# Gather of a mixture-of-experts stage: rows stored feature part by feature part, slots in two halves of 320 columns

## The reference, cut to what matters

```
def grouped_moe(x, router_w, router_bias, w_gate_up, w_down):
    scores = jax.nn.sigmoid(t @ router_w)
    ...
    h = jnp.einsum('td,edf->tef', t, w_gate_up)
    a = silu(h[..., :D_EXPERT]) * h[..., D_EXPERT:] * gates[..., None]
    y = jnp.einsum('tef,efd->td', a, w_down)
```

## Time and profile before

| | |
|---|---|
| median of 3 runs | 1055.7 us (1053.37 to 1056.87) |
| profiled execution, its own time | 1055.6 us |
| its span | 1053.8 us |
| mean granted clock of TensorE | 0.994 |
| PE busy | 1024.5 us, 97% |
| VectorE busy | 659.8 us, 63% |
| ScalarE busy | 533.5 us, 51% |
| chain that ended last | PE 87%, DVE 5% |

### The profile page before, as it was taken

How to read it: one execution, slowest core, us unless ns; L and a number is a source line. 1 busy time by engine, 2 the same in 40 slices (tenths; PEclk the granted TensorE clock), 3 DMA queues, 4 the chain that set the end, 5 groups by cost and what they waited for, 6 DMA issues and landing times.

```text
span 1053.8 us, 14257 instructions
## 1 busy us (share of the span) xinstructions
PE 1024.5 (97%) x5876; PEld 863.9 (82%) x5876; DVE 659.8 (63%) x760; ACT 533.5 (51%) x649; POOL 92.1 (9%) x75
## 2 busy tenths in 40 slices
PE   8999899999999999998999999999999999999998
PEld 8997558888888889975588888888899758999997
DVE  2105655799999571065557999996748635645644
ACT  3344423677777333444236777775458544334331
POOL 0370000000000013650000000000003100000000
PEclk9999999999999999998999999999999999999999
DMA  9900921499999539028214999994141634454441
GB/s 272 299 26 21 379 80 41 161 401 381 367 367 381 146 88 262 1 55 355 80 41 159 407 383 360 373 388 171 74 160 39 232 130 160 161 214 183 166 145 47
DMA packets 93303, 214.89 MB, mean 204 GB/s; under 512 B 25248, under 2 KB 56112, under 8 KB 82880
## 3 DMA queue, kind: packets, MB, share of 16 engines
q1 hardware_dynamic: 91456, 209.40, 55.4%
q0 software_dynamic: 1504, 2.73, 1.1%
q10 hardware_dynamic: 288, 1.98, 0.5%
HBM read 213.05 MB, written 1.05 MB: 203 GB/s over the span
## 4 chain that ended last, share of the span: by engine, by line
PE 87%; DVE 5%; SPq 3%; DMA 1%; ACT 1%; issue 1%; POOL 1%; DVEq 0%; ACTq 0%
PE bank L1095 77%; PE bank L1136 2%; DMA WE<-in_w_in 1%; SPq L526 1%; POOL QL L635 1%; PE bank L1188 1%; DVE X L1681 1%; DVE small L1673 1%; DVE X L1685 1%; PE bank L1462 1%; DVE X L1671 1%; PE bank L1170 1%; PE bank L1149 1%; PE bank L1164 1%; SPq L510 0%
## 5 line engine op out<-in xcount | busy, mean ns | idle before, releaser
L1825 DVE TENSOR_TENSOR BL<-WE,BH 128x2048 fp32r<-128x2048 f32 x120 | 273.6, 2290 | 24.7 <-ACT BH L785 22.8
L785 ACT CAST BH<-WE 128x2048 fp32r<-128x2048 f32 x120 | 228.9, 1909 | 43.8 <-PE bank L1095 43.8
L1095 PE MATMUL bank<-BH,XS_ALL 128*128 128x512 f32 x512 | 163.0, 390 | 0.0
L1095 PEld LDWEIGHTS bank<-BH,XS_ALL 128*128 128x128 f32 x512 | 96.2, 188 | 19.9
L1095 PE MATMUL bank<-BL,XS_ALL 128*128 128x512 f32 x256 | 99.6, 389 | 0.0
L635 POOL TENSOR_TENSOR QL<-WE,QH 128x2048 fp32r<-128x2048 f32 (+2 forms) x12 | 49.3, 4123 | 366.6 <-ACT QH L777 366.6
L1095 PE MATMUL bank<-WB,XT 128*128 128x512 f32 x160 | 70.4, 595 | 3.2 <-ACT XT L853 1.4
L1095 PE MATMUL bank<-XTH,WH 128*128 128x256 f32 x256 | 72.6, 284 | 0.8 <-DVE XTL L1979 0.8
L1095 PE MATMUL bank<-XTL,WH 128*128 128x256 f32 x256 | 72.4, 283 | 0.0
L1095 PE MATMUL bank<-XTH,WL 128*128 128x256 f32 x256 | 72.4, 283 | 0.0
L1136 PE MATMUL bank<-tab 128*128 128x128 f32 x492 | 62.1, 285 | 5.0 <-DMA tab<-in_tables 5.0
(11 more groups left out here) (338 smaller groups left out, 2275.4 us busy)
## 6 DMA issues: line engine op xcount, KB each, us to landing
WE<-in_exp_w_gate_up SPq DMA_DIRECT2D x80, 1024.0 KB, 7.3
WE<-in_exp_w_down SPq DMA_DIRECT2D x40, 1024.0 KB, 7.4
WE<-in_w_up SPq DMA_DIRECT2D x16, 1024.0 KB, 5.2
WE<-in_w_down SPq DMA_DIRECT2D x16, 1024.0 KB, 5.7
WE<-in_w_in SPq DMA_DIRECT2D x7, 2048.0 KB, 8.4
WE<-in_w_in SPq DMA_DIRECT2D x8, 1024.0 KB, 8.3
WB<-in_w_out SPq DMA_DIRECT2D x2, 2560.0 KB, 9.9
WE<-in_w_in SPq DMA_DIRECT2D x12, 256.0 KB, 7.6
```

The lines of the kernel that those rows point to most:

```text
L785: nc.scalar.copy(BH[b % N_PAIR][:, :], raw[b % N_RAW]).then_inc(blk_high[b % N_PAIR], 1)
L1095: ins = nc.tensor.matmul(dst, lhsT, rhs, start=first and n == 0, stop=last and n == len(pairs) - 1)
L1825: v.tensor_tensor(BL[b % N_PAIR][:, :], raw[b % N_RAW], BH[b % N_PAIR][:, :].bitcast(F32), ALU.subtract).then_inc(blk_low[b % N_PAIR], 1)
```

## The change

X1H and X1L get a layout of part k by j, so that the 128 columns that one matmul takes as weights lie side by side; ScalarE's copy and VectorE's subtraction now read X with a step of eight words. SEL's columns get a new order: two halves of 320 (groups 0 and 1 with the first 64 over slots, groups 2 and 3 with the other 64), and behind them once more the 128 over slots, for the transposes and the gates. VectorE writes SEL in four operations for each tile instead of one. The gather makes jobs `ga{k}` and `gb{k}` of 320 columns in banks 2, 3, 4, 6 and 7, with four matmuls each, instead of `g{k}` and `go`. ScalarE and VectorE evacuate each job with two operations, of 256 and 64 columns. The expert stage's waits name the new jobs.

```
-    ("g0", 2), ("g1", 3), ("g2", 4), ("g3", 2), ("g4", 3), ("g5", 4), ("g6", 2), ("g7", 3), ("go0", 6), ("go1", 7),
+    ("ga0", 2), ("gb0", 3), ("ga1", 4), ("gb1", 6), ("ga2", 7), ("gb2", 2), ("ga3", 3), ("gb3", 4),
+    ("ga4", 6), ("gb4", 7), ("ga5", 2), ("gb5", 3), ("ga6", 4), ("gb6", 6), ("ga7", 7), ("gb7", 2),
...
+SEL_HALF = N_GRP // 2 * P + P // 2
+def slot_columns(g):
+    at = 2 * SEL_HALF if g == N_GRP else g // 2 * SEL_HALF + g % 2 * P
+    return slice(at, at + P)
...
-        X1H, X1L = over("X1H", "WB", 0, [P, T, D]), over("X1L", "WB", UNIT, [P, T, D])
-        SEL = over("SEL", "XT", 0, [P, T, N_SLOT * P])
+        X1H, X1L = over("X1H", "WB", 0, [P, T, KD, P]), over("X1L", "WB", UNIT, [P, T, KD, P])
+        SEL = over("SEL", "XT", 0, [P, T, 2 * SEL_HALF + P])
...
+        def feature_blocks(t):
+            return X[:, t, :].rearrange("p (j k) -> p k j", k=KD)
...
-                    nc.scalar.copy(X1H[:, t, :], X[:, t, :]).then_inc(rows_high, 1)
+                    nc.scalar.copy(X1H[:, t, :, :], feature_blocks(t)).then_inc(rows_high, 1)
...
-                for half in range(2):
-                    for k in range(4 * half, 4 * half + 4):
-                        act.wait_ge(*full(f"g{k}", l))
-                        dst = XS_ALL[:, :].rearrange("p (g q) -> p g q", g=N_GRP)[:, :, k * P:(k + 1) * P]
-                        nc.scalar.copy(dst, bank(f"g{k}")[:, :].rearrange("p (g q) -> p g q", g=N_GRP)).then_inc(gathered, 1)
-                    act.wait_ge(*full(f"go{half}", l))
-                    nc.scalar.copy(XS[N_GRP][:, half * 512:(half + 1) * 512], bank(f"go{half}")[:, :]).then_inc(gathered, 1)
-                    selection_T(half)
+                def gather_high(k, half):
+                    job = f"g{'ab'[half]}{k}"
+                    act.wait_ge(*full(job, l))
+                    dst = XS_ALL[:, :].rearrange("p (g q) -> p g q", g=N_GRP)[:, 2 * half:2 * half + 2, k * P:(k + 1) * P]
+                    nc.scalar.copy(dst, bank(job)[:, 0:2 * P].rearrange("p (g q) -> p g q", g=2))
+                    at = k * P + half * HD
+                    nc.scalar.copy(XS[N_GRP][:, at:at + HD], bank(job)[:, 2 * P:SEL_HALF]).then_inc(gathered, 1)
+                for k in range(KD):
+                    for half in range(2):
+                        gather_high(k, half)
+                    if k % 4 == 3:
+                        selection_T(k // 4)
...
                 product(ranks[:, 2 * N_GRP:3 * N_GRP], [(ones, first_tile), (ones, second_tile)]).then_inc(*made("rank"))
-                keep_warm("g0", l, 10)
+                keep_warm("ga0", l, 10)
                 pe.wait_ge(rows_low, (l + 1) * T)
                 pe.wait_ge(sel_made, (l + 1) * T)
                 def gather(dst, k, cols):
                     return product(dst, [pair for t in range(T) for pair in (
-                        (X1H[:, t, k:D:KD], SEL[:, t, cols]), (X1L[:, t, k:D:KD], SEL[:, t, cols]))])
+                        (X1H[:, t, k, :], SEL[:, t, cols]), (X1L[:, t, k, :], SEL[:, t, cols]))])
                 def selection_T(n, block, i):
-                    return nc.tensor.transpose(tile_of(f"selT{n}", block, P), SEL[:, i % 2, (i // 2) * P:(i // 2 + 1) * P].bitcast(F32), ident)
+                    return nc.tensor.transpose(tile_of(f"selT{n}", block, P), SEL[:, i % 2, slot_columns(i // 2)].bitcast(F32), ident)
                 def slot_gates(g):
                     at = 2 * P + g * PER_GRP
                     return product(bank("selT2")[:, at:at + PER_GRP], [
-                        (SEL[:, t, g * P:(g + 1) * P].bitcast(F32), gov[:, t, :]) for t in range(T)])
+                        (SEL[:, t, slot_columns(g)].bitcast(F32), gov[:, t, :]) for t in range(T)])
                 for n in range(3):
                     pe.wait_ge(*free(f"selT{n}", l))
                 for k in range(KD):
                     half = k // 4
-                    pe.wait_ge(*free(f"g{k}", l))
-                    gather(bank(f"g{k}")[:, :], k, slice(0, N_GRP * P)).then_inc(*made(f"g{k}"))
-                    if k % 4 == 0:
-                        pe.wait_ge(*free(f"go{half}", l))
-                    ins = gather(tile_of(f"go{half}", k % 4, P), k, slice(N_GRP * P, N_SLOT * P))
-                    if k % 4 == 3:
-                        ins.then_inc(*made(f"go{half}"))
+                    for part in range(2):
+                        job = f"g{'ab'[part]}{k}"
+                        pe.wait_ge(*free(job, l))
+                        gather(bank(job)[:, 0:SEL_HALF], k, slice(part * SEL_HALF, (part + 1) * SEL_HALF)).then_inc(*made(job))
                     ins = selection_T(half, k % 4, k)
                     if k % 4 == 3:
                         ins.then_inc(*made(f"selT{half}"))
...
                     for part, kind in enumerate(("A", "B")):
                         b = BLOCK_AT[kind, n]
                         pe.wait_ge(*rested(b, l))
-                        if n == 0:
+                        if n % (2 * PER_GRP) == 0:
                             for k in range(4 * part, 4 * part + 4):
-                                pe.wait_ge(*read(f"g{k}", l))
-                        elif n == N_GRP * PER_GRP:
-                            pe.wait_ge(*read(f"go{part}", l))
+                                pe.wait_ge(*read(f"g{'ab'[n // (2 * PER_GRP) % 2]}{k}", l))
                         high, low = (w[b % N_PAIR][:, :].rearrange("p (k n) -> p k n", k=KD // 2) for w in (BH, BL))
                         for k in range(KD // 2):
                             kk = 4 * part + k
...
                     evacuate(f"x1T{n}", XT[:, 2 * n:2 * n + 2, :], l)
                 for t in range(T):
                     dve.wait_ge(rows_high, l * T + t + 1)
-                    v.tensor_tensor(X1L[:, t, :], X[:, t, :], X1H[:, t, :].bitcast(F32), ALU.subtract).then_inc(rows_low, 1)
+                    v.tensor_tensor(X1L[:, t, :, :], feature_blocks(t), X1H[:, t, :, :].bitcast(F32), ALU.subtract
+                                    ).then_inc(rows_low, 1)
                 dve.wait_ge(router_in, 32)
...
                 link(v.tensor_reduce(posm[:, :, N_GRP], posm[:, :, 0:N_GRP], AX.X, ALU.add))
                 link(v.tensor_scalar(posm[:, :, N_GRP], posm[:, :, N_GRP], float(-P), None, ALU.add))
                 for t in range(T):
-                    v.tensor_tensor(SEL[:, t, :].rearrange("p (g q) -> p g q", g=N_SLOT), spread(tb("place"), 1, [P, N_SLOT, P]),
-                                    spread(posm[:, t, :], 2, [P, N_SLOT, P]), ALU.is_equal).then_inc(sel_made, 1)
+                    halves = SEL[:, t, 0:2 * SEL_HALF].rearrange("p (h c) -> p h c", h=2)
+                    for h in range(2):
+                        v.tensor_tensor(halves[:, h, 0:2 * P].rearrange("p (g q) -> p g q", g=2), spread(tb("place"), 1, [P, 2, P]),
+                                        spread(posm[:, t, 2 * h:2 * h + 2], 2, [P, 2, P]), ALU.is_equal)
+                    v.tensor_scalar(halves[:, :, 2 * P:SEL_HALF], tb("place").rearrange("p (h q) -> p h q", h=2),
+                                    posm[:, t, N_GRP:N_SLOT], None, ALU.is_equal)
+                    v.tensor_scalar(SEL[:, t, 2 * SEL_HALF:], tb("place"), posm[:, t, N_GRP:N_SLOT], None, ALU.is_equal
+                                    ).then_inc(sel_made, 1)
                 link(v.tensor_tensor(esel, esel, sc.rearrange("p (g e) -> p g e", e=4), ALU.mult))
...
                 link(v.tensor_reduce(gov, esel.rearrange("p (t g) e -> p t e g", t=T), AX.X, ALU.add))
                 v.tensor_tensor(gov, gov, spread(gden, 2, [P, T, PER_GRP]), ALU.mult).then_inc(gates_ready, 1)
-                def gather_low(dst, high, src, job, n):
-                    dve.wait_ge(gathered, l * 10 + n + 1)
-                    v.tensor_tensor(dst, src, high.bitcast(F32), ALU.subtract).then_inc(*took(job))
-                xs4 = XS_ALL[:, :].rearrange("p (g q) -> p g q", g=N_GRP)
+                def gather_low(k, half):
+                    job = f"g{'ab'[half]}{k}"
+                    dve.wait_ge(gathered, l * 2 * KD + 2 * k + half + 1)
+                    xs = XS_ALL[:, :].rearrange("p (g q) -> p g q", g=N_GRP)[:, 2 * half:2 * half + 2, :]
+                    v.tensor_tensor(xs[:, :, D + k * P:D + (k + 1) * P], bank(job)[:, 0:2 * P].rearrange("p (g q) -> p g q", g=2),
+                                    xs[:, :, k * P:(k + 1) * P].bitcast(F32), ALU.subtract)
+                    at = k * P + half * HD
+                    v.tensor_tensor(XS[N_GRP][:, D + at:D + at + HD], bank(job)[:, 2 * P:SEL_HALF],
+                                    XS[N_GRP][:, at:at + HD].bitcast(F32), ALU.subtract).then_inc(*took(job))
                 for k in range(KD):
-                    gather_low(xs4[:, :, D + k * P:D + (k + 1) * P], xs4[:, :, k * P:(k + 1) * P],
-                               bank(f"g{k}")[:, :].rearrange("p (g q) -> p g q", g=N_GRP), f"g{k}", k + k // 4)
-                    if k % 4 == 3:
```

(5 more changed lines are left out.)

## The result

The changed kernel takes 1044.2 us (median of 5 runs, 1043.38 to 1045.48); the kernel before, 1053.37 us in five runs (1052.4 to 1056.87). The ratio is 0.9903 with a 95% interval of 0.9885 to 0.9921: faster by about 1%, 8 to 12 us. The profiled execution has a span of 1042.1 us.

The account below looks back on a forecast made before the run. It took TensorE as the bound, busy 1024.5 of 1053.8 us, with strided weight loads pacing the gather. Per layer 5.5 saved less 0.5 for SEL gives 5.0, over two layers 10.0: 1055.6 to 1045.6 us, range 1042 to 1050.

Parts of the forecast that it names:

- likeliest case: Whole kernel: the forecast itself, 10.0 us saved over two layers, giving 1045.6 us; chance 0.68.
- The weight load's step sets the pace: Gather: loads at every eighth word take 334 ns against 188 contiguous; rival that layout has no effect, 1056.6 us, chance 0.04.
- 0.147 us for 320 columns: Gather on TensorE: price of each new 320-column product; rival of dear 320 columns, 1062.6 us, chance 0.04.
- The straight line between 256 and 512: TensorE: 320-column price interpolated between 0.120 us for 256 columns and 0.228 us for 512.
- 5.5 us a layer out of the stage: Gather on TensorE: eight k at 0.70 us less each, minus 0.12 for dearer transposes at k = 6 and 7.
- SEL 0.5 us longer: VectorE ahead of the gather: eight SEL operations instead of two cost 0.5 us a layer, range 0.3 to 0.6.
- The split's strided read is hidden: ScalarE and VectorE before the router: strided reads cost nothing, covered by 1.0 us; rival that it hurts, 1050, chance 0.09.
- The sign of being wrong: The prediction would be wrong if row splitting ran beyond 4 us.
- Evacuation keeps up: ScalarE and VectorE: 0.59 and 0.63 us a job against TensorE's 0.65; rival that evacuation sets pace, 1048.4, chance 0.10.
- The expert stage keeps the gain: Expert stage: moves earlier with TensorE, pieces still 8.43 us apart; rival that weight stream bounds it, no change, chance 0.05.

Follow-up runs that it names:

- the layout alone: The kernel before with only the new contiguous layout of X1H and X1L, jobs of 512 and 128 columns and SEL as before: 1045.3 us, ratio 0.9908.
- the halves alone: The whole change with X1H and X1L feature by feature as before, read with a step of eight words: 1055.9 us, ratio 1.0007.
- 384 and 256: The whole change with SEL in its old order, one operation a tile, and jobs of 384 and 256 columns: 1040.9 us, ratio 0.9875.
- the experiment that used it up: The whole change with the low part of the second tile's rows computed three times on VectorE: 1048.6 us in one run.
- the two kernels with slow loads: The whole change with X1H and X1L feature by feature as before (ratio 1.0007), and the whole change with parts stored in fours (1056.6 us).

## Why the prediction was right

It gave 1045.6 us, a range of 1042 to 1050, and 1043.5 to 1047.5 for its likeliest case; measured were 1044.2, and by the account of the stages 10.3 us saved where it had 10.0. The mechanism held in each part. That the sum is so close is partly luck: the stage gave 0.3 us a layer more than assumed, and SEL took 0.16 back. The other 1.1 us down to the measured median fit its starting point: the profile of 1055.6 us is one in which both untouched stretches took their longer time (18.80 and 100.60 us), and the median of the five runs before is 1053.37.

- *The weight load's step sets the pace*: right, shown by the layout alone (14.00 us a stage) and by the halves alone (19.10).
- *0.147 us for 320 columns*: right (178.42, 178.57, 178.72). The straight line between 256 and 512 held, and 384 columns fit it too (0.174).
- *5.5 us a layer out of the stage*: 5.81. One k saves 0.71 us, and 0.73 where the gates' products are in it, not 0.70: a transpose left 0.11 us, not 0.12, and the gates' products add 0.44, not 0.46. These are in the stream from k = 3 on (180.44 to 182.89 before), not from k = 4 as the prediction read; five k have them instead of four, and since they cost nearly the same before and after, the sum hardly moves.
- *SEL 0.5 us longer*: 0.66, just outside its 0.3 to 0.6. The price of the 256-column operations was right at 421 ns, the full one, though they don't read PSUM; a 128-column one takes 0.28 us, not 0.25, and is followed after 0.20 us, not 0.17.
- *The split's strided read is hidden*: right, with factor 2.0 on ScalarE and 1.67 for VectorE's pair (3.92 against 2.35 us), where 2.03 was assumed for both. The factor was taken over from TensorE's loads, and that it fits ScalarE so well is luck. The cover left on VectorE is 1.88 us, not 1.0, and the experiment that used it up paid for what went beyond it. The sign of being wrong, a split beyond 4 us, was set too tight: 3.92 us came close to it with the cover still there.
- *Evacuation keeps up*: right, and by more than the 0.02 us that a sum without overlap left: 0.58 us a job.
- *The expert stage keeps the gain*: right, 8.43 us a unit as before.
- What it didn't ask is which half of the change earns it. Layout alone has 4.46 of the 5.15 us. The halves take another 1.35 out of the stage and give 0.66 back in SEL.

## What to carry to other kernels

When products of very different widths start at the same distance, look at the weight load, and at the step between its columns before its size: a step of two fp32 words (8 bytes) was nearly as good as contiguous columns here, a step of four was not. Whoever moves a stride from a tight engine to others should look up the idle time that these have before their next deadline, and count it as a budget. And a split of columns that keeps the old order of the tables (384 and 256) got the same stage as two equal halves, without paying for new ones.

## What the runs showed of the hardware beyond that

- A weight load of 128 fp32r columns: 188 to 189 ns contiguous, 196 at 8 bytes from column to column, 330 at 16, 334 to 339 at 32. Back to back, with a product of few enough columns between, loads follow every 0.11 us when contiguous (128 columns), every 0.23 us at 16 bytes and every 0.24 at 32.
- The granted clock fell in the middle of a busy stage, in the first layer of the two kernels with slow loads and a 1.1 us idle time ahead: 0.66 and 0.77 of full speed in two stretches of 3 us with strided columns; 0.86 and 0.58 at 16 bytes. In the second layer of both, with the same loads and the same idle time, it stayed at 1.00. Before, with the same loads and 0.46 us of idle time, it stayed at 1.00, and so did the change, with 1.11 us idle and fast loads. So neither the loads nor the idle time is enough by itself, nor are both together always; what decides wasn't tried.
